# Two-layer hybrid trunk, one core: the end of the HGRN2 recurrence and the output projection in another order

## What is computed

```
# HGRN2, one chunk of 64 tokens, forward and backward in time
attn = sum_k q k decay
out  = (q * exp(cum)) @ state  +  attn @ v
new_state = state * exp(c_last) + (k * exp(c_last - cum))^T @ v
...
# after both directions, for the delta-rule heads and the HGRN2 heads
y = rms(o) * norm_w * silu(z)
...
y = concat([attention, deltanet, hgrn2]) @ w_out
x = x + m[2] * y
h = rms(x) * (1 + m[4]) + m[3]      # rows that the experts gather
```

## Time and profile before

| | |
|---|---|
| median of 3 runs | 3473.76 us (3472.07 to 3474.4) |
| the profiled execution, its own time | 3467.72 us |
| its span | 3465.6 us |
| PE busy | 2956.5 us, 85% |
| DVE busy | 2287.9 us, 66% |
| ACT busy | 1829.1 us, 53% |
| bytes moved | 686.61 MB, mean 198 GB/s |

### The profile page before, as it was taken

One profiled execution on the slowest core, in us unless ns is written; L12 is line 12 of the kernel. 1 busy time (PEld: TensorE's weight loads), 2 busy tenths in 40 slices (PEclk: granted clock), 3 DMA queues, 4 the chain that ended last, 5 costly groups with the idle time before them and its releaser, 6 DMA issues.

```text
span 3465.6 us, 61217 instructions
## 1 busy us (share of the span) xinstructions
PE 2956.5 (85%) x24987; PEld 2277.8 (66%) x24987; DVE 2287.9 (66%) x2940; ACT 1829.1 (53%) x2450; POOL 330.2 (10%) x98
## 2 busy tenths in 40 slices
PE   8999987877868999999995999877576789888897
PEld 1788876744536676667764898767453677766676
DVE  1362766577346788887875545656754788888887
ACT  1224521223236787777774335322233688888886
POOL 0000000000001121122110000000000122222212
PEclk9999998888878999999997999878567899999998
DMA  9122011041146999999994211000014799999996
GB/s 347 51 68 78 1 39 51 15 136 50 49 195 243 359 352 354 370 354 351 364 368 167 63 61 37 2 2 3 2 50 175 277 376 379 384 371 367 380 380 254
DMA packets 212697, 686.61 MB, mean 198 GB/s; under 512 B 16011, under 2 KB 74611, under 8 KB 212369
## 3 DMA queue, kind: packets, MB, share of 16 engines
q1 hardware_dynamic: 198020, 644.16, 49.1%
q0 software_dynamic: 6144, 20.98, 2.6%
q10 hardware_dynamic: 8335, 18.56, 1.4%
HBM read 662.62 MB, written 21.02 MB: 197 GB/s over the span
## 4 chain that ended last, share of the span: by engine, by line
PE 58%; DVE 14%; ACT 11%; issue 9%; DMA 7%; SPq 0%; ACTq 0%; DVEq 0%; POOL 0%
PE ps L872 11%; PE ps L2282 10%; PE ps L2252 9%; PE ps L1585 6%; PE ps L2020 4%; ACT hi L2360 4%; DMA gu<-in_moe_w_up 3%; DVE gu_lo L2506 3%; PE ps L1267 3%; ACT arena L2369 2%; DMA gu<-in_moe_w_gate 2%; PE ps L792 2%; PE ps L2290 2%; PE ps L1898 2%; PE ps L1923 1%
## 5 line engine op out<-in xcount | busy, mean ns | idle before, releaser
L2506 DVE TENSOR_TENSOR gu_lo<-gu,hi 128x2816 fp32r<-128x2816 f32 x256 | 781.8, 3086 | 222.2 <-ACT hi L2360 199.7
L2360 ACT ACTIVATE hi<-gu 128x2816 fp32r<-128x2816 f32 x256 | 644.6, 2551 | 175.0 <-DMA gu<-in_moe_w_up 124.3
L2252 PE MATMUL ps<-hi,xsplit 128*96 128x512 f32 (+3 forms) x2304 | 565.9, 392 | 40.3 <-DVE arena L2520 15.8
L2252 PEld LDWEIGHTS ps<-hi,xsplit 128*96 128x96 f32 (+1 forms) x2304 | 398.7, 178 | 155.1 <-ACT hi L2360 30.1
L2506 DVE TENSOR_TENSOR down_lo<-down,hi 128x1024 fp32r<-128x1024 f32 (+1 forms) x256 | 401.5, 1618 | 65.9 <-ACT hi L2360 65.9
L2252 PE MATMUL ps<-gu_lo,xsplit 128*96 128x512 f32 (+3 forms) x1536 | 386.5, 388 | 39.6 <-DVE gu_lo L2506 39.4
L2360 ACT ACTIVATE hi<-down 128x1024 fp32r<-128x1024 f32 (+1 forms) x256 | 343.5, 1379 | 122.1 <-PE ps L2282 122.1
L2252 PEld LDWEIGHTS ps<-gu_lo,xsplit 128*96 128x96 f32 (+1 forms) x1536 | 268.1, 181 | 131.8 <-DVE gu_lo L2506 71.2
L1585 PE MATMUL ps<-arena 64*64 64x64 f32 (+1 forms) x6080 | 207.9, 226 | 33.6 <-DVE arena L1341 21.5
L1585 PEld LDWEIGHTS ps<-arena 64*64 64x64 f32 x6080 | 198.3, 138 | 42.0 <-DVE arena L1341 24.3
L2592 POOL DMA_INDIRECT arena<-xn_rows,row_of x32 | 32.7, 1021 | 1864.8 <-DMA xn_rows<-arena 1037.7
(11 more groups left out here) (326 smaller groups left out, 5024.9 us busy)
## 6 DMA issues: line engine op xcount, KB each, us to landing
gu<-in_moe_w_gate SPq DMA_DIRECT2D x256, 704.0 KB, 9.0
gu<-in_moe_w_up SPq DMA_DIRECT2D x256, 704.0 KB, 6.8
down<-in_moe_w_down SPq DMA_DIRECT2D x64, 2048.0 KB, 13.9
down<-in_moe_w_down SPq DMA_DIRECT2D x32, 1536.0 KB, 17.2
arena<-in_w_mod SPq DMA_DIRECT2D x12, 2048.0 KB, 17.6
arena<-in_w_in SPq DMA_DIRECT2D x22, 1024.0 KB, 5.2
arena<-in_w_mod SPq DMA_DIRECT2D x15, 1024.0 KB, 5.2
arena<-in_w_mod SPq DMA_DIRECT2D x18, 512.0 KB, 3.8
```

What stands on the lines that cost most here:

```text
L2252: ins = nc.tensor.matmul(ps[0:lhs.shape[1], 3 * m + b, 0:n], lhsT=lhs, rhs=w[:, c0 + 512 * b:c0 + 512 * b + n], start=(row == 0 and stage ...
L2360: nc.scalar.activation(hi_part(p, is_last), whole(p), ACT.Copy).then_inc(hi_a.sem, 1)
L2506: nc.vector.tensor_tensor(lo_part(p), whole(p), hi_part(p, is_last).bitcast(F32), ALU.subtract) \
```

## The change

- The inner products of all tiles move ahead of the wait for `hstate`, into three banks (4 to 6). At `d` = 0 ScalarE copies them into `ycat`, and VectorE adds the state products onto it. At `d` = 1 VectorE adds both as before.
- At `d` = 1 TensorE also turns column groups 0 to 3 ahead of that wait, and ScalarE copies them (`act_turned`). Groups 4 and 5 and the spreading of the gates stand ahead of the wait for `mixed`.
- The gates are multiplied by the norms' weights at `d` = 0 ahead of the states (`weigh_gates`), not in `dve_gated`.
- The squares of the HGRN2 heads are made on ScalarE, one tile at a time.
- The root is one Sqrt on ScalarE and a reciprocal on VectorE, where there were Ln and Exp, in the gated norms and in the norm of the projection's rows.
- `x` and `xn2` are stored tile by tile (512 KB each) on ACT's queue.

```diff
             link(nc.vector.tensor_reduce(ss[:, s0:24], sqg[:, i0:].rearrange("p i (h d) -> p (i h) d", d=HD), AX, ALU.add))
...
         def act_gated(act, layer, which):
             act.wait_ge(go_ss.sem, go_ss.n(layer, which + 1))
             s0 = 4 * out_from(layer)
-            link_act(nc.scalar.activation(rs[:, s0:24], ss2[:, s0:24], ACT.Ln))
-            nc.scalar.activation(rs[:, s0:24], rs[:, s0:24], ACT.Exp, scale=-0.5).then_inc(go_rs.sem, 1)
+            nc.scalar.activation(rs[:, s0:24], ss2[:, s0:24], ACT.Sqrt).then_inc(go_rs.sem, 1)
...
                 if d == 0:
                     dve_squares(dve, layer, 0, 512)
+                    weigh_gates(layer, 0, dz[:, :, 0:256])
+                    link(weigh_gates(layer, 1, hgt[:, :, 256:512]))
...
+                if d == 0:
+                    act.wait_ge(hout.sem, hout.n(layer, 1))
+                    for n, i in enumerate(out_tiles(layer)):
+                        nc.scalar.activation(ycat[:, i, 768:1024], ps[:, 4 + n // 2, 256 * (n % 2):256 * (n % 2) + 256],
+                                             ACT.Copy).then_inc(go_sq.sem, 1)
+                else:
+                    for f in range(4):
+                        act_turned(act, layer, f, 2 * (f % 2))
+                    for n, i in enumerate(out_tiles(layer)):
+                        act.wait_ge(houtv.sem, houtv.n(layer, len(out_tiles(layer)) + n + 1))
+                        nc.scalar.activation(sqg[:, i], ycat[:, i, 768:1024], ACT.Square).then_inc(go_sq.sem, 1)
                 act_gated(act, layer, d)
...
+                outs = list(out_tiles(layer))
+                for n, i in enumerate(outs):
+                    for h in range(DNH):
+                        for par in range(2):
+                            c0 = 256 * (n % 2) + HD * h
+                            ins = nc.tensor.matmul(ps[HB[par], 4 + n // 2, c0:c0 + HD], lhsT=Ah[HB[par], h, i, :],
+                                                   rhs=hgt[HB[par], i, h * HD:(h + 1) * HD], start=True, stop=True)
+                ins.then_inc(hout.sem, 1)
+                if d == 1:
+                    pe.wait_ge(uhev.sem, uhev.n(layer, 12))
+                    for f in range(4):
+                        if f >= 2:
+                            pe.wait_ge(yt_a.sem, yt_a.n(layer, f - 1))
+                        turn_columns(layer, f, 2 * (f % 2))
                 pe.wait_ge(hstate.sem, hstate.n(layer, d + 1))
...
-                link_act(nc.scalar.activation(rs[:, i:i + 1], ss2[:, i:i + 1], ACT.Ln))
-                nc.scalar.activation(rs[:, i:i + 1], rs[:, i:i + 1], ACT.Exp, scale=-0.5).then_inc(act_rs.sem, 1)
-                if n == len(outs) - 1:
-
-                    rows_at, keep = (x_rows, NT) if layer < DEPTH - 1 else (t["out"][0], NT_LAT)
-                    act.dma_start(rows_at.rearrange("(i p) d -> p i d", p=P), x[:, NT - keep:NT, :]).then_inc(x_out.sem, 16)
-                    act.wait_ge(normed.sem, normed.n(layer, NT + n + 1))
-                    act.dma_start(xn_rows[0:len(outs) * P, :].rearrange("(i p) d -> p i d", p=P), xn2[:, outs[0]:NT, :]) \
-                        .then_inc(xn_out.sem, 16)
+                nc.scalar.activation(rs[:, i:i + 1], ss2[:, i:i + 1], ACT.Sqrt).then_inc(act_rs.sem, 1)
+                rows_at = x_rows if layer < DEPTH - 1 else t["out"][0]
+                act.dma_start(rows_at[n * P:(n + 1) * P, :], x[:, i, :]).then_inc(x_out.sem, 16)
+                act.wait_ge(normed.sem, normed.n(layer, NT + n + 1))
+                act.dma_start(xn_rows[n * P:(n + 1) * P, :], xn2[:, i, :]).then_inc(xn_out.sem, 16)
...
+                link(nc.vector.reciprocal(rs[:, i:i + 1], rs[:, i:i + 1]))
                 nc.vector.tensor_scalar(xn2[:, i, :], x[:, i, :], rs[:, i:i + 1], None, ALU.mult).then_inc(normed.sem, 1)
```

103 lines of the change are left out of this document (57 added, 46 removed).

## The result

The changed kernel takes 3426.06 us in the median of 4 runs (3422.62 to 3428.39), and the kernel before took 3472.91 us beside it (3466.7 to 3474.4, 4 runs). The ratio is 0.9871, with a 95% interval of 0.9855 to 0.9887. The profiled execution took 3422.62 us (span 3420.8 us), 45.1 us less than the profiled one before, where the sum said 33.8.

The account below looks back on a forecast made before the run. No engine bounds the whole span: experts' stretch and projection are full, the rest short chains of waits. Layer 0's 22.3 and layer 1's 11.5 make 33.8 us, 3433.9 profiled, 3440 as median; range for 8 in 10 3427 to 3451.

Parts of the forecast that it names:

- the terms 6.0 and 2.5: Last sum to projection: the `w_out` landing limits the gain to its spare, 6.0 us in layer 0, 2.5 in layer 1.
- The experts absorb it: Experts' stretch timed by its weight stream, so up to half the gain stays there: 3457, worst case 3472; chance 0.06.
- the gather keeps its wait: Gather behind routing: last rows queue with weights or its transfer meets remaining loads; the 7.0 go, 3447; chance 0.12.
- slower: Projection: TensorE idles some 4 us for `w_out`, stays at the lower clock, projection takes up to twice as long; chance 0.02.
- the mechanism that I gave 0.48: The forecast itself, all steps over both layers, with a range of its own of 3434 to 3446; chance 0.48.
- signs of being wrong: Projection starting at VectorE's last copy; clock 1.00 in d = 0 products; gather awaiting `xn_rows`; states ending before transposes; longer experts.
- with two sets of banks a tile takes (0.92 + 0.67 + 0.5 + 0.1)/2 = 1.1 us: Tiles behind the states at d = 0, TensorE at the lower level: end at 794.3, 2.6 us less in layer 0.
- 3.6, 3.3, 3.3 and 3.3: Gains in us taken for the tiles: d = 0 in layers 0 and 1, then d = 1 in layers 0 and 1.
- TensorE keeps its upper level: Tiles, and transposes and logits behind the last tile: work under the states keeps the clock up; 43 us, 3431; chance 0.17.
- I cost it at nothing, and at 1.3 us if it is exposed: Softmax behind the last tile: its Exp needs its own table load, 1.28 us, while ScalarE waits for VectorE's row maxima.
- The fourth rival: Work under the states too long at the lower clock: products 4 us late in layer 0, 0.6 in layer 1; 3445; 0.07.
- the old distance from `mixed` to VectorE's last copy (4.0 us): Ahead of the projection in layer 0: `mixed` at 882.6 plus this unchanged distance makes the columns ready at 886.6.

Follow-up runs that it names:

- filler: Kernel before plus 48 matmuls (32 in layer 1) ahead of the states' wait in each direction; d = 0 stretch to last sum 18.93 and 17.82 us.
- old norm: Changed kernel with the gated norms' squares in one VectorE product and root by Ln and Exp; last sum to projection 15.33 and 13.57 us.
- both versions: Two kernels: changed kernel with earlier `w_out` loads, less gate spreading in layer 1, an early softmax table load; medians 3417.71 and 3416.06 us.
- turned early: Changed kernel with earlier `w_out` loads, less layer 1 spreading, early softmax table load, column groups 4 and 5 also turned under the states; 3417.71 us.
- the early Exp: Changed kernel plus an unused one-column Exp ahead of the first expert's weights; last product to end of routing 31.57 and 29.91 us.
- the second version: Changed kernel with earlier `w_out` loads, less layer 1 spreading, early softmax table load, no column groups turned under the states; median 3416.06 us.

## Why the prediction was right, and where its sizes were wrong

**Right, by its steps.** The first matmul stands 13.91 and 13.43 us behind the last sum, where 13.3 and 13.6 were forecast, and the terms 6.0 and 2.5 came out as 5.46 and 2.69. `mixed` came 7.1 us behind the last sum (forecast 7.0), the gather 0.29 us behind routing (7.04 us gained for 7.0), no table load was left between squares and roots of the projection's tiles, the gates' products fitted ahead of the states to 0.1 us. "The experts absorb it", "the gather keeps its wait" and "slower" did not happen: the stretch of the experts moved with its start, within its own scatter. So the mechanism that I gave 0.48 is in the main the one that the runs show, and 11.6 us were missing in its sizes (45.4 in the seven stretches for 33.8). Two of my signs of being wrong came true with it, both in layer 0: the projection started at VectorE's last copy, and the products of d = 0 began at a clock of 1.00.

**The tiles, 6.4 us of it.** The step that failed is "with two sets of banks a tile takes (0.92 + 0.67 + 0.5 + 0.1)/2 = 1.1 us", and with it 3.6, 3.3, 3.3 and 3.3. Measured on the table's stretches: 6.04, 5.44, 4.24 and 4.17. The 0.67 of handover were read off a first tile of 2.5 us at the lower level, less the pitch of 1.83 of its products; but a handover takes 0.06 us (the products at 865.98 take 0.46, VectorE starts at 866.50; the profile models the ends of matmuls, so this is their modelled end). And 8 products take 0.70 us at the lower level, not 0.92. So two tiles take 1.3 us even there (1.31 in layer 1), nearly what I had granted to the upper level alone (0.6 a tile). At d = 1 VectorE sets the pace, as forecast, with 0.85 us a tile and not 0.93. I had asked which clock level the tiles would see. Layer 1 at d = 0 showed that this matters little: all its tiles ran at the lower level and gained the 5.4 us of my sum for the upper one. Putting the inner products back (14.9 us) showed that their place was worth three quarters of the gain, the level at which they run included. The last quarter, fewer sums and banks that are free sooner, is argued and not shown. The rival "TensorE keeps its upper level" named 43 us, nearer to the 45 than my sum, but by luck: the clock was up only at the start of the tiles in layer 0 and down in layer 1, and 5.0 of the 45 us came from transfers that it didn't name.

**The transfers behind the projection, 5.0 us.** I costed the gather's own transfer as unchanged. It became 2.1 and 2.9 us shorter, since the bulk stores had shared the queues with it; putting them back cost 3.1 and 3.1. This was the term that was missing altogether. The rows had it: in layer 1 routing and gather were already together before, and yet the store by tile takes 3 MB out of the traffic behind the last tile (4 MB stored, of which the last tile's 1 MB stays).

**The clock in the projection, 1.7 us.** 0.70 and 0.98 us came in the projection itself, where I had nothing. Its first matmuls in layer 0, before and after:

```profile
898.30:904.30 6.00, 5.99 (x7) 2.50 (x8) 0.00 (x0) 0.00 (x0) 0.00 (x0) 0.50 0.00 0
```

```profile
885.60:890.20 4.60, 4.53 (x6) 1.98 (x7) 0.00 (x0) 0.00 (x0) 0.00 (x0) 0.50 0.00 0
```

Half of the time at the lower level is lost, and that accounts for all of it. The projection of layer 0 took 98.56, 97.86, 97.20 (filler), 97.17 (old norm) and 95.62 us (both versions) with 5.9, 4.5, 3.2, 3.1 and 0 us of its start at 0.50; that of layer 1 took 65.71, 64.73, 64.89 (turned early) and 62.83 us with 5.8, 3.8, 4.2 and 0. The kernel with the bulk stores, which has none under the projection, lies on the same line (97.91 with 4.6), so the stores under it cost nothing.

**The last tile, 1.2 us less than forecast.** "I cost it at nothing, and at 1.3 us if it is exposed": it was exposed by 0.57 and 1.29, as the early Exp showed. Without that, 2.4 and 3.1 us would stand against the 2.4 forecast. In layer 1 it matters little, since the gathered rows came only 0.15 us sooner without it. The fourth rival's 3445 covers its late products (4.6 us) alone; with the tables' 2.6 it would have been 3447.

**The norm and the start of the projection, 0.4 us less in all.** The reason given, that the transfer alone decides, holds in layer 1 (1.5 us with half the bytes) and not in layer 0 (nothing), where the near hit, 13.91 for 13.3, is in part luck. There TensorE's own chain is as late, because it runs at the lower level: I had taken "the old distance from `mixed` to VectorE's last copy (4.0 us)" and found 2.3 us to spare, and never costed the spreading's 7.19 us ahead of that wait. That the early transposes "end in that wait" was right for layer 1 (0.1 us); in layer 0 they are worth as little (0.2 us), there with the clock's help.

What stays open: why the clock comes back 4 us into the changed kernel's projection, and ahead of it in both versions in layer 0 but only in the second in layer 1; where the rest of the 2.1 and 1.9 us behind d = 0 went with the inner products put back; and how much of the projection's start before the change was luck of the clock, since filler work alone moved it by 3 us.

## What to carry to other kernels

Work that needs nothing from a serial chain belongs ahead of the wait for it. But price a pipeline's pace by the pitch between its tiles, with the handover read from two rows of both engines, and not by what is left of a first tile. When a store or load is taken out of a crowded stretch, ask of every other transfer there what it gains, not only of the one that waited. And where several chains end within a microsecond of each other (transfer, transposes at the lower level, copies behind a root in an in-order queue), shortening one can buy nothing; the next gain came from the transfer's issue, the spreading and the clock together.

## What the runs showed of the hardware

- The granted clock follows TensorE's work late, in both directions. With 24 transposes moved from under the states to behind the last sum, it fell sooner and was back sooner, and in layer 0 the projection started where it had (14.08 for 13.91 us), since the spreading fell from 7.19 to 3.79 us.
- The same instructions in the same order can start 3 us later when only filler work some 20 us earlier differs (22.50 against 19.37 us from the last sum to the projection of layer 0, with the clock at 0.50 throughout).
- What a stretch full of matmuls loses to the clock is half of its time at the lower level, to 0.1 us in eleven projections.
- A 2 MB load of `w_out` that has the queues to itself lands in 7.8 us (the second version's last load in layer 1); the second of two issued together in 12.8 to 13.1.
- Stores of 512 KB under the projection landed in 2.7 us in the median and cost no time on any engine that was waited for. The Trainium skill ("DMA: Bandwidth & Descriptors", section on bandwidth) asks for 1 MiB and more a transfer, from loads that it measured. Here the smaller stores cost nothing, since the projection hides them, and their early end is the gain.
